# Projecting the two gate inputs and the shared rotary key of the even layer as one piece of 96 columns

## The reference

```
EVEN_IN_SIZES = (256, 256, 512, 2*16, 512, 256, 128, 32, 512)
gq, gk, gv, glr, gg, cq, ckv, kr, mg = split_cols(h @ w_in, EVEN_IN_SIZES)
lr_dirs = jnp.split(glr, 2, axis=-1)                # two gate inputs of 16
g[d] = log_sigmoid(lr_dirs[d] @ w2[d] + b[d]) / 16  # decays, d = 0, 1
k_rot = apply_rope(kr, cos, sin)                    # one rotary key of 32 for all heads
```

## Time and profile before

| what | value |
|---|---|
| median of 3 runs | 2534.51 us (2528.3 to 2535.52) |
| the profiled execution's span | 2530.5 us, mean granted clock 0.959 |
| TensorE busy | 2328.4 us (92%), 11068 matmuls |
| VectorE busy | 1529.0 us (60%) |
| ScalarE busy | 1187.9 us (47%) |
| GpSimd busy | 373.4 us (15%) |

### The profile page before, as it was taken

How to read it: one execution, slowest core, us unless ns; L and a number is a source line. 1 busy time by engine, 2 the same in 40 slices (tenths; PEclk the granted TensorE clock), 3 DMA queues, 4 the chain that set the end, 5 groups by cost and what they waited for, 6 DMA issues and landing times.

```text
span 2530.5 us, 27448 instructions
## 1 busy us (share of the span) xinstructions
PE 2328.4 (92%) x11068; PEld 1719.4 (68%) x11068; DVE 1529.0 (60%) x1877; ACT 1187.9 (47%) x1669; POOL 373.4 (15%) x258
## 2 busy tenths in 40 slices
PE   6988789798699999999989999898999998899998
PEld 5766555475488888888768676554555467778876
DVE  5766157544799999999771024746555647533475
ACT  3255256521388888888662044425444432312231
POOL 2000012000111111111100000011555534000014
PEclk9999899898899999999989998998999999899999
DMA  3201010116899999999751010010000032111141
GB/s 118 67 31 37 0 67 1 67 75 256 347 372 379 384 379 404 391 393 380 273 184 46 1 51 1 1 38 1 1 1 34 17 125 75 37 66 50 44 161 53
DMA packets 98874, 342.08 MB, mean 135 GB/s; under 512 B 21276, under 2 KB 46661, under 8 KB 71096
## 3 DMA queue, kind: packets, MB, share of 16 engines
q1 hardware_dynamic: 87096, 318.76, 33.6%
q0 software_dynamic: 10448, 17.28, 1.8%
q10 hardware_dynamic: 1200, 4.24, 0.4%
HBM read 323.41 MB, written 33.60 MB: 141 GB/s over the span
## 4 chain that ended last, share of the span: by engine, by line
PE 81%; DVE 9%; ACT 5%; DMA 2%; issue 2%; SPq 0%; DVEq 0%; POOL 0%; ACTq 0%; POOLq 0%
PE psm L230 78%; DVE mem L953 1%; PE psm L1722 1%; ACT mem L1143 1%; DMA mem<-in_ada_w_dram 1%; PE psm L1073 1%; DVE r L337 1%; DMA mem<-in_w_in_dram 1%; DVE mem L2741 1%; PE psm L1745 1%; PE psm L464 1%; ACT mem L1109 1%; DMA mem<-in_odd_w_out_dram 1%; DVE small L3008 0%; DVE r L3264 0%
## 5 line engine op out<-in xcount | busy, mean ns | idle before, releaser
L230 PE MATMUL psm<-r,r 128*128 128x512 f32 (+4 forms) x7438 | 1777.5, 397 | 76.4 <-DVE r L337 17.9
L230 PEld LDWEIGHTS psm<-r,r 128*128 128x128 f32 (+3 forms) x7438 | 1380.6, 189 | 472.0 <-issue 63.7
L337 DVE TENSOR_TENSOR r<-mem,r 128x1024 fp32r<-128x1024 f32 x448 | 525.8, 1221 | 174.7 <-ACT r L328 169.5
L328 ACT ACTIVATE r<-mem 128x1024 fp32r<-128x1024 f32 x448 | 441.1, 1052 | 33.5 <-DMA mem<-in_w_in_dram 22.1
L230 PE MATMUL psm<-mem 128*64 128x128 f32 (+13 forms) x2230 | 358.8, 437 | 34.7 <-ACT mem L816 9.1
L230 PEld LDWEIGHTS psm<-mem 128*64 128x64 f32 (+6 forms) x2230 | 167.9, 163 | 155.7 <-issue 88.7
L3216 POOL TENSOR_TENSOR mem<-mem 128x1024 f32<-128x1024 f32 x63 | 153.9, 2443 | 177.6 <-ACT mem L3171 176.9
L3171 ACT ACTIVATE mem<-psm 128x512 f32<-128x512 f32 x160 | 95.4, 597 | 148.5 <-PE psm L230 141.1
L3008 DVE TENSOR_REDUCE small<-psm 128x1 f32<-128x1280 f32 x64 | 95.2, 1488 | 104.6 <-PE psm L230 104.2
L230 PE MATMUL psm<-mem,cst 128*128 128x512 f32 (+4 forms) x274 | 115.1, 638 | 23.3 <-ACT mem L924 5.5
L265 ACT ACTIVATE small<-small 128x1 f32<-128x1 f32 (+3 forms) x26 | 7.7, 295 | 236.1 <-DVE small L374 151.0
(11 more groups left out here) (338 smaller groups left out, 1774.7 us busy)
## 6 DMA issues: line engine op xcount, KB each, us to landing
mem<-in_exp_w_gate_dram SPq DMA_DIRECT2D x64, 1024.0 KB, 7.4
mem<-in_exp_w_up_dram SPq DMA_DIRECT2D x64, 1024.0 KB, 7.6
mem<-in_exp_w_down_dram SPq DMA_DIRECT2D x64, 1024.0 KB, 7.3
mem<-in_ada_w_dram SPq DMA_DIRECT2D x16, 1024.0 KB, 14.0
mem<-in_odd_w_in_dram SPq DMA_DIRECT2D x10, 1024.0 KB, 5.3
mem<-in_even_w_in_dram SPq DMA_DIRECT2D x9, 1024.0 KB, 5.3
mem<-in_x_dram SPq DMA_DIRECT2D x16, 512.0 KB, 7.1
mem<-in_w_in_dram SPq DMA_DIRECT2D x8, 1024.0 KB, 5.3
```

Of the source, the lines that this page charges most:

```text
L230: return p.e.matmul(o, l, r, start=start, stop=stop, skip_group_check=True)
L328: p.e.activation(h, mem(kb + 8, [R * n])[:, w * q:w * q + w], ACT.Copy).then_inc(*self.hi_done.up(i, q))
L337: p.e.tensor_tensor(l, mem(kb + 8, [R * n])[:, w * q:w * q + w], h.bitcast(F32), SUB).then_inc(*self.lo_done.up(i, q))
```

## The change

The weight piece that held `ckv`, `kr` and the gate inputs (192 columns) becomes one of 224: `ckv` (128), then columns 1024 to 1055, 1040 to 1071 and the 32 of `kr`. The last 96 form one piece "lkr" with the layout of `LK`: rows 0 to 15 and 32 to 47 are the two gate inputs, 64 to 95 the rotary key; rows 16 to 31 and 48 to 63 are filled too, and nobody reads them. "lk" twice and "lr" go, "lkr" is projected once, after "ckv". The piece comes by four DMAs in place of two. On ScalarE and VectorE the halving of the next piece (`split(p, 6)`) now stands behind the "ckv" tiles.

```diff
-                     (SA, [(w_e[:, :, 1824:1984], 0, 160), (w_e[:, :, 1024:1056], 160, 32)], 8, 192),
+                     (SA, [(w_e[:, :, 1824:1952], 0, 128), (w_e[:, :, 1024:1056], 128, 32), (w_e[:, :, 1040:1072], 160, 32),
+                           (w_e[:, :, 1952:1984], 192, 32)], 8, 224),
...
-        plain = [("cq", j, o) for j in range(2) for o in (256, 768)] + [("lk", k, o) for k in range(2) for o in (0, 256, 768)] + \
-                [("ckv", 0, o) for o in (0, 256, 768)] + [("lr", 0, o) for o in (0, 256, 768)] + \
+        plain = [("cq", j, o) for j in range(2) for o in (256, 768)] + [("ckv", 0, o) for o in (0, 256, 768)] + \
+                [("lkr", 0, o) for o in (0, 256, 768)] + \
...
-            if name == "lk":
-                return LK[32 * j:32 * j + 16, o:o + n]
             if name == "ckv":
                 return CKV[:, o:o + n]
-            if name == "lr":
-                return LK[64:96, o:o + n]
+            if name == "lkr":
+                return LK[0:96, o:o + n]
...
-            for k in range(2):
-                by_channels_tensor(p, "lk", k, 5, 160 + 16 * k, 16, True, none)
             by_channels_tensor(p, "ckv", 0, 5, 0, 128, True, none)
-            WV.frees(5, by_channels_tensor(p, "lr", 0, 5, 128, 32, True, none))
+            WV.frees(5, by_channels_tensor(p, "lkr", 0, 5, 128, 96, True, none))
...
-            for k in range(2):
-                by_channels(p, who, "lk", k, 16, True, none)
+            by_channels(p, who, "ckv", 0, 128, True, none)
             split(p, 6)
-            by_channels(p, who, "ckv", 0, 128, True, none)
-            by_channels(p, who, "lr", 0, 32, True, none)
+            by_channels(p, who, "lkr", 0, 96, True, none)
```

More of the change, by code:

```diff
@@ L2335, in latents_scalar @@
         def latents_scalar(p):
-            p.wait_ge(*ev_pe.at("lr", 0, 768))
+            p.wait_ge(*ev_pe.at("lkr", 0, 768))
             for name in ("cq", "ckv"):
@@ L2386, in lk_there @@
         def lk_there(p):
[L2387 to L2390, removed]
+            for key in turn_by:
+                if key[0] == "lkr":
+                    p.wait_ge(*(ev_dve if turn_by[key] == "vector" else ev_act).at(*key))
         def rise_free(p, u):
```

## The result

| | before | after |
|---|---|---|
| device time, median of 4 runs | 2531.49 us (2528.3 to 2535.52) | 2506.3 us (2504.7 to 2512.31) |
| ratio, 95% interval | | 0.9901 [0.9884, 0.9918] |
| profiled execution: span | 2530.5 us | 2503.5 us |
| its own time | not shown | 2505.39 us |

The kernel is 1.0% faster: 25.2 us by the medians, 27.0 us by the two profiled spans. The forecast was 24.85 us less, 2509.6 us.

A forecast was written before the change was run, and what follows sets the result against it. TensorE alone was taken to bound the touched stage. 27.75 + 0.1 - 2.5 - 0.5 = 24.85 us less than the 2530.5 us span gives 2505.6; with 4.0 around the span, 2509.6 us, range 2503 to 2517.

The forecast's parts named there:

- The bound: From the first "mg" tile to the end of the gate tiles, only TensorE sets the pace, without a wait.
- What goes: In the small projections on TensorE, two passes of 72 matmuls go: 27.75 us by the wall, 28.4 by busy time.
- The width: In the "lkr" tiles, 96 channels in place of 32 cost from -0.2 to +0.1 us; a gain of 0.1 taken.
- Weight loads hidden: In the "lkr" tiles, 96-column loads of about 162 ns stay hidden; unhidden, 72 loads would cost 3.8 us.
- Larger halving, more DMAs: Under the "cq" tiles, halving of some 1.8 and 2.1 us and two more DMAs fit in 8.3 us spare: cost 0.
- The new wait: Around the first decay, shifted PSUM banks make the second gate tile wait and start 2.5 us late; bounds 0 and 4.4.
- The clock behind it: In the gate tiles after the wait, a longer half-clock stretch costs 0.5 us, priced between -1.7 and +1.0.
- The sum: Whole kernel: 24.85 us less, giving a span of 2505.6 and, with 4.0 around it, 2509.6 us.
- no new wait: Around the first decay, the bank ring shifts but both waits are already met: 2506.7 us; chance 6%.
- Unhidden loads: In the "lkr" tiles, weight loads come out from under the matmuls: 3.8 us worse, 2513.4 us; chance 3%.
- the wait for weights: Behind "lkr", weight pieces arrive no earlier, so freed time becomes waiting and the time stays about 2534 us; chance 3%.
- the slow clock: In the remaining gate tiles, the clock stays at its lower level: 36.6 us more, 2545.7 us; chance 2%.

The follow-up runs named there:

- e4: The kernel before with only the two gate inputs merged into one pass of 48 columns, later tiles in their old PSUM banks: 2519.17 us, ratio 0.9947.
- e7: The changed kernel with the bank ring advanced by six and the weight piece padded from 224 to 256 columns: 2505.51 us, ratio 0.9897.
- e12: The changed kernel, bank ring advanced by six, piece padded to 256 columns, "lkr" projected with 128 output columns in place of 96: 2505.05 us in one run.
- e8: The changed kernel, bank ring advanced by six, its weight piece halved behind the second "cq" part instead of the first: 2509.27 us, ratio 0.9905.
- e1: The changed kernel with the PSUM bank ring advanced by six behind the "cq" tiles, so later tiles keep their old banks: 2505.21 us, ratio 0.9890.
- e2: The kernel before, nothing merged, with the bank ring advanced by two so tiles lie in the changed kernel's banks: 2533.47 us, ratio 1.0013.
- e3: The changed kernel with the bank ring advanced by one, the second gate tile in the last rise chunk's bank: 2514.63 us, ratio 0.9932.
- e9 to e11: The changed kernel with 6, 12 and 18 extra matmuls ahead of the first "cq" tile: 2509.97, 2509.03 and 2508.57 us.
- e6: The same program as e1, run once more: 2506.84 us, ratio 0.9905.

## Why the prediction was right

- **The bound.** Right: the stage ran on TensorE alone, so work taken out of it came out of the end of the stage.
- **What goes, 27.75 us.** Measured 27.59 with the width (e4: half of it is 13.83). Right, and the wall time per tile was the better source than the busy sum of 28.4.
- **The width, a gain of 0.1 us.** Wrong in sign and too small to matter. I took "ckv" tiles to keep their 5.46 us and a 96-channel tile to lie nearer to them than to the 32-channel one. Both kinds took 5.56 (e7, e12 show why, in part). It is a loss of 0.16 us (27.75 against 27.59), just beyond the 0.1 that I had given as its bound, and it sits in the "ckv" tiles, which I had at nothing: an "lkr" tile took the 5.56 us of the 32-channel one.
- **Weight loads hidden.** Right. The row for the new width:

```profile
L230 PEld LDWEIGHTS psm<-r,r 128*96 128x96 f32 x72 | 10.6, 162 | 3.3
```

  162 ns is what the line between 32 and 128 columns gave. The rule of the Trainium skill ("TensorE: Matmul & The Clock Gate", "LDWEIGHTS (loading the stationary operand)"), that a load takes its columns divided by 1.2, in ns, agrees in slope: (162 - 109) / 64 = 0.83 ns a column. It does not agree in size: it gives 80 ns for 96 columns where the trace has 162, so the prediction's "agrees" holds for the slope alone. The load ends in no price here: "lkr" tiles took 5.56 us with it and "lr" tiles 5.56 with loads of 109 ns.
- **Larger halving, more DMAs: 0.** Right. 1.80 and 2.08 us as forecast. No single landing took longer (5.9 us at most, where 6.4 stood), but the last of the five issues starts at 1382.7, where the last of three started at 1380.1, so the piece as a whole did come later: ScalarE waited 0.18 us for a DMA at 1384.95, where it had not waited, some 15 us before TensorE needed the piece. e8 shows what the missing cover would have cost, 4.6 us in the stage.
- **The new wait, 2.5 us.** Right in mechanism, place and size. The second gate tile starts at 1493.62; without the waits it would start at 1518.85 - 27.69 = 1491.16, so 2.46 us late. e1 takes the wait away, e2 makes it in the kernel before, e3 makes it larger. One detail was off: the gap ahead of the gate tile is 1.10 us, not 1.6, since rise itself took 2.94 instead of 2.41.
- **The clock behind it, 0.5 us.** The "gg" column is 3.01 longer, 2.46 of it wait: 0.55. The half-clock stretch went from 3.4 to 4.7 us, which halved is 0.65. Right in size, though e9 to e11 show that it comes out between 0 and 0.9 for one and the same wait, so the 0.55 was partly luck.
- **The sum.** At the end of the gate stage 24.68 us, forecast 24.85. What the sum left out is everything behind that stage: the span of the profiled execution fell by a further 2.3 us in stages that the change doesn't touch, for which I had only a bound of 1 us for bank shifts. The other small miss is the time around the span: I carried 4.0 us over, and it was 1.9 (2505.39 against 2503.5). By medians the gain is 25.2 us, 0.35 from the forecast. The forecast time lies 3.3 us above the median after, and 3.0 of these are that the median before moved from 2534.51 (3 runs) to 2531.49 (4 runs). That the gain by medians comes so near is in part luck, since untouched stages moved by 2.5 us between two executions of one program.

The rivals: "no new wait" (6%) fell to [1.10 <-DVE mem L2456], although its time, 2506.7, is nearer to the median than mine: the total alone would have picked the wrong mechanism. Unhidden loads (3%) fell to the tile times, the wait for weights (3%) to the fetch and halving rows, the slow clock (2%) to the 4.7 us of its stretch, and "the merge saves nothing" (1%) to the time itself.

A better version was tried on the way: the old banks (e1, e6) and wider rows (e7, e12) take 3.0 us out of the gate stage and 0.3 out of the stretch ahead of it in the traces. None is faster than the changed kernel in the total.

## What to carry to other kernels

Small projections of the same input cost a full pass each, whatever their output channels: put them side by side into one pass as long as the columns fit one weight, and look for where the consumers need them. Removing tiles from a ring of PSUM banks moves every tile behind them into another bank: look up the new tenants where a second user has fixed banks, since such meetings cost 3.0 us of the gate stage here and 6.4 with the ring one bank further on. Judge an edit of 3 us by its own stretch of the trace, with the untouched stretches beside it, since these moved by 2.5 us between two executions of one program.

## What the runs showed of the hardware

- After a pause of TensorE the length of the half-clock stretch is not given by the pause: in two executions of one program, after 2.13 us each, the mean granted clock of the next 2.91 us was 1.00 and 0.68, and after 1.63 and 1.64 us the next 168 matmuls took 39.9 to 40.9 us.
- The granted clock also fell without a pause: in the kernel before it was 0.51 for 3.4 us behind the six matmuls of "rise" (2.41 us, contracting over 16 rows), with TensorE busy throughout.
- A tile of 24 fp32r matmuls with 512 columns took 5.44 us with 128 output channels read from rows of 192 or 256 weight columns and 5.56 from rows of 224; with 96 output channels it took 5.52 from rows of 256 and 5.56 from rows of 224.
- A weight load of 96 columns took 162 ns and was hidden: the tile took the same 5.56 us as with loads of 32 columns and 109 ns.
- With two more strips to fetch, the narrowest 32 columns wide, no landing took longer (5.9 us at most, against 6.4), but the issues took until 1382.7 in place of 1380.1, and ScalarE waited 0.18 us for the piece.
